# Moving all SBUF tiles of a two-block transformer kernel: first address 17,408 instead of 16,512

## The reference

```python
hx = modulate(rmsnorm(x, norm1_g), mx[0], mx[1])      # mx, mc = silu(c) @ ada_w + ada_b
hc = modulate(rmsnorm(ctx, norm1_g), mc[0], mc[1])
ux, uc = hx @ w_in, hc @ w_in                         # 1024 -> 5120
sc_f, sc_b = gated scan states of the context         # from uc
ox = gated scan of ux in both directions, from these states
ya = fourier_mix(ux[:512]) @ w_a
yb = readout(ux, ox) @ w_b
x = x + mx[2] * ((sigmoid(ga) * ya + sigmoid(gb) * yb) @ w_out)
h2 = modulate(rmsnorm(x, norm2_g), mx[3], mx[4])
z = depthwise_conv3x3(h2 @ ffn_up) + conv_b           # 1024 -> 5632, on a grid of 4 x 64
x = x + mx[5] * ((silu(z[:2816]) * z[2816:]) @ ffn_down)
x = rmsnorm(x, final_g)
```

```python
p = rms_norm(x, norm1_g_2) @ w_in_2                   # 1024 -> 2560
q, k = rms_norm(q), rms_norm(k)
mix = [softmax attention with a bias, gated short convolution, windowed means]
x = x + mix @ w_out_2
f = square(relu(rms_norm(x, norm2_g_2) @ w_mlp1))     # 1024 -> 4096
x = x + f @ w_mlp2
```

## The kernel before

| tile | address | modulo 1,024 | modulo 64 |
|---|---|---|---|
| `raw0` | 16,512 | 128 | 0 |
| `whi0` | 49,280 | 128 | 0 |
| `wlo0` | 73,856 | 128 | 0 |
| `XR` | 98,432 | 128 | 0 |
| `vec` | 113,280 | 640 | 0 |
| `RR` | 121,696 | 864 | 32 |
| `base` (all areas) | 123,872 | 992 | 32 |

## Time and profile before

### The profile page before, as it was taken

How to read it: one execution, slowest core, us unless ns; L and a number is a source line. 1 busy time by engine, 2 the same in 40 slices (tenths; PEclk the granted TensorE clock), 3 DMA queues, 4 the chain that set the end, 5 groups by cost and what they waited for, 6 DMA issues and landing times.

```text
span 762.5 us, 14142 instructions
## 1 busy us (share of the span) xinstructions
PE 739.1 (97%) x5852; PEld 717.0 (94%) x5852; DVE 491.2 (64%) x907; ACT 358.6 (47%) x452; POOL 398.5 (52%) x223
## 2 busy tenths in 40 slices
PE   7779999999999989999999999999899999999998
PEld 3679889999999989999999999999899999999997
DVE  3877797569526559777777764548655656556553
ACT  5586224245434555554555546346454433334331
POOL 0767553546648957878878877766585300000000
PEclk9999999999999989999999999999999999999999
DMA  9984886337534437555455544433435464464411
GB/s 362 417 360 162 344 304 262 140 111 244 207 110 159 166 117 294 177 188 200 167 170 199 184 167 166 166 112 111 148 133 203 181 220 165 169 216 160 176 57 56
DMA packets 21089, 145.84 MB, mean 191 GB/s; under 512 B 2465, under 2 KB 2977, under 8 KB 3746
## 3 DMA queue, kind: packets, MB, share of 16 engines
q1 hardware_dynamic: 20880, 144.87, 51.8%
q10 hardware_dynamic: 146, 0.07, 0.0%
HBM read 143.88 MB, written 1.05 MB: 190 GB/s over the span
## 4 chain that ended last, share of the span: by engine, by line
PE 90%; DVE 4%; ACT 4%; issue 2%; DMA 0%; DVEq 0%; ACTq 0%
PE bank L1426 24%; PE bank L1428 24%; PE bank L1427 24%; PE bank L1444 3%; PE CP L1428 2%; PE CP L1426 2%; PE CP L1427 2%; PE bank L1533 2%; PE bank L1469 1%; ACT SCR L793 1%; ACT whi L487 1%; PE bank L1484 1%; DVE GA L1119 1%; PE CP L1458 0%; PE bank L1642 0%
## 5 line engine op out<-in xcount | busy, mean ns | idle before, releaser
L469 POOL TENSOR_TENSOR wlo<-raw,whi 128x512 fp32r<-128x512 f32 (+1 forms) x201 | 377.8, 1910 | 170.6 <-ACT whi L487 170.5
L487 ACT ACTIVATE whi<-raw 128x2048 fp32r<-128x2048 f32 x103 | 196.3, 1907 | 43.7 <-PE bank L1428 29.2
L1186 DVE SCALAR_TENSOR_TENSOR Y<-bank,vec,Y 128x189 f32<-128x189 f32 (+2 forms) x352 | 123.0, 423 | 43.6 <-ACT Y L734 43.6
L1426 PE MATMUL bank<-H2h,whi 128*128 128x256 f32 x352 | 101.0, 287 | 1.7 <-DVE H2l L1161 1.7
L1427 PE MATMUL bank<-H2l,whi 128*128 128x256 f32 x352 | 100.6, 286 | 0.0
L1428 PE MATMUL bank<-H2h,wlo 128*128 128x256 f32 x352 | 99.8, 284 | 0.0
L1426 PE MATMUL bank<-H1h,whi 128*128 128x256 f32 (+1 forms) x288 | 90.9, 316 | 8.3 <-DVE H1l L917 4.5
L1428 PE MATMUL bank<-H1h,wlo 128*128 128x256 f32 (+1 forms) x288 | 89.2, 310 | 0.0
L1427 PE MATMUL bank<-H1l,whi 128*128 128x256 f32 (+1 forms) x288 | 89.0, 309 | 0.0
L850 DVE TENSOR_TENSOR wlo<-raw,whi 128x2048 fp32r<-128x2048 f32 x28 | 64.4, 2300 | 34.5 <-ACT whi L487 34.5
L1426 PE MATMUL bank<-H4h,whi 128*128 128x256 f32 x256 | 72.6, 284 | 0.0
(11 more groups left out here) (326 smaller groups left out, 1878.9 us busy)
## 6 DMA issues: line engine op xcount, KB each, us to landing
raw<-in_w_mlp SPq DMA_DIRECT2D x32, 1024.0 KB, 4.8
raw<-in_w_in SPq DMA_DIRECT2D x30, 1024.0 KB, 5.7
raw<-in_ffn_up SPq DMA_DIRECT2D x22, 1024.0 KB, 4.9
raw<-in_ada_hi SPq DMA_DIRECT2D x16, 1024.0 KB, 4.9
raw<-in_ffn_down SPq DMA_DIRECT2D x11, 1024.0 KB, 4.8
raw<-in_w_out SPq DMA_DIRECT2D x8, 1024.0 KB, 4.8
ada_s<-in_ada_s SPq DMA_DIRECT2D x4, 1024.0 KB, 18.1
ada_p<-in_ada_p SPq DMA_DIRECT2D x2, 1024.0 KB, 10.2
```

The costliest lines, as they stand in the source:

```text
L469: m = e.tensor_tensor(l[:, a:a + step], r[:, a:a + step], h[:, a:a + step].bitcast(F32), ALU.subtract)
L487: e.activation(whi[q % NHI][:, :], raw[n % NRAW][:, :], ACT.Copy).then_inc(s["w_hi"], 1)
L1186: e.scalar_tensor_tensor(o[:, r0:r1, c0:c1], z[:, r0 + dr:r1 + dr, c0 + dc:c1 + dc], cw[:, f, tap:tap + 1], o[:, r0:r1, c0:c1], ALU.mult, ...
L1426: e.matmul(out, h[:, col:col + P], xh, start=first, stop=False, skip_group_check=True)
```

## The change

`start` goes from 16,512 to 17,408, and `base` is rounded up to the next multiple of 1,024:

```diff
@@ -175,7 +175,7 @@
-    start = 16512
+    start = 17408
     cursor = [start]
@@ -216,7 +216,7 @@
     GS = keep("GS", [P, KT])
-    base = cursor[0]
+    base = (cursor[0] + 1023) // 1024 * 1024
```

## The result

| | before | after |
|---|---|---|
| median of 20 runs | 764.90 us | 767.86 us |
| range | from 763.85 us | 765.14 to 769.11 us |
| ratio of the runs | | 1.0032 [1.0026, 1.0039] |
| profiled execution, span | 764.52, 762.5 us | 765.14, 763.1 us |

The forecast was 732.8 us, with a range from 724 to 767 and 0.12 on slower. The time lies outside the range, on the other side of before. One run of before took 943.3 us and one beside the experiments 1,199.9 us; both are left out of what follows.

A forecast was written before the change was run, and what follows sets the result against it. PE bounds the kernel through the distance between matmuls. Gains of 29.0, 2.6 and 0.8 us less 0.5 for GpSimd sum to 31.9 us, taken from 764.5 or 764.9 to give 732.8 us; range 724 to 767.

The forecast's parts named there:

- What bounds the kernel: Whole kernel: PE, busy 739.1 of 762.5 us; matmul distance 120.0 ns, 13.3 of it set by the streaming operand's address.
- (a) Activations: Streamed tiles in mm3 and by_tokens: moving from 32 to 0 modulo 64 gains 29.0 + 2.6 + 0.8 us.
- seventeenth 64-byte block: Streaming reads: a run starting 32 bytes into a block touches 17 blocks, not 16, costing 6.7 ns per run.
- The 0.5 us taken back for GpSimd: Eight chunks of w_a, w_b and w_out: GpSimd's 5.50 us per chunk would bind against PE's 5.44, costing 0.5 us.
- (b) Weight buffers: Weight buffers and XR, moved by 896 bytes: bits this high show no effect on the pace, so nothing taken.
- (c) DMA: First 38 us, queues full: nothing taken, at most 2.5 us; the skill's 256-byte rule would give 1.2 us.
- (d) The other engines: VectorE, ScalarE, GpSimd: none but GpSimd at 233:268 near full in bound stretches; only softmax could show change; nothing taken.
- Rival 2: All matmuls: the change does nothing to PE, two reads cost 120.0 ns whatever their address; 764.9 us, chance 0.20.
- Rival 3: mm3: streaming and stationary reads collide when starting in step, about 125 ns; 21.7 us slower, 787 us, chance 0.12.
- Rival 1: mm3 and by_tokens: alignment helps only to by_tokens' pace, 117.3 ns for both streams; 752 us, chance 0.13.

The follow-up runs named there:

- e9: The changed kernel with GpSimd's last chunk (w_mlp1 3) given to VectorE and base 64 bytes back; median 743.70 us, ratio 0.9714.
- e8: The changed kernel with GpSimd's last chunk (w_mlp1 3) given to VectorE and base 512 bytes on; 764.22 us.
- e12: The changed kernel with GpSimd's last chunk (w_mlp1 3) given to VectorE and base 256 bytes on; 765.98 us.
- e3: The kernel before with only base rounded up, by 32 bytes to 123,904, start left at 16,512; 764.26 us, ratio 1.0000.
- e1: The changed kernel run once more, nothing else altered; 768.10 us, ratio 1.0041.
- e16: The kernel before with start 16,544 and base 96 bytes behind the last tile, last chunk left with GpSimd; median 751.73 us, ratio 0.9783.
- e2: The kernel before with only start moved to 17,408, base following unrounded; 764.92 us, ratio 1.0002.

## Why the prediction was wrong

**What bounds the kernel** was right: PE, by the distance between starts, 120.0 ns where 106.7 are columns. That the address of the streaming operand sets it was right in kind. e9 shows what was there to win: 2.9%, with 113.3 ns in all but some 140 us of its profiled execution.

**(a) Activations, -32.4 us: the step that failed.** I laid a line through two overheads (13.3 for one run, 20.0 for two), read its slope as a seventeenth 64-byte block, and let it go with the shift. Two points always lie on a line, and nothing in the trace tested the reading: all tiles shared one offset. The measured terms are 4,346 x 0.0 = 0 us for the 256-column form, 192 x -6.6 ns = -1.3 us for the 512-column form (forecast -2.6), and 192 x +2.6 ns = +0.5 us for the bound `by_tokens` (forecast -0.8). 0.8 us of gain in place of 32.4. I had written that if the 512-column form did not fall by twice as much, the picture was wrong; here one fell and the other did not move. The 0.5 us taken back for GpSimd in 233:268 did not arise either, there being no faster PE to wait for it.

**(b) Weight buffers, nothing.** "Bits this high show no effect" looked at 128 against 640, which differ by 512. That difference is indeed without effect (e8, e12). But the shift was by 896, which is 128 modulo 256, and the streams moved by 1,056, which is 32: D went from 96 to 0 modulo 256. I priced the two shifts one by one where only their difference counts. That the time still came out near nothing is because 96 and 0 both give 120.0 ns (as 128 does in part, e3).

**(c) DMA, nothing.** Right. 364 and 416 GB/s became 366 and 420, the shares 0.90 and 1.00 for 0.91 and 1.01. 1% on 38 us is 0.4 us at most. The Trainium skill's rule on 256 bytes (DMA: Bandwidth & Descriptors, "How a descriptor splits into AXI transactions") would have given 1.2 us. The traces of before and after do not show it. That section speaks of bytes that are fetched from below the start, and the change moved only the side in SBUF, where the rows are written; the estimate passed over that.

**(d) The other engines, nothing.** This is the second failed step, and the sign of the result hangs on it. I looked for engines that are full over a stretch. The loss lies in a stretch where GpSimd works for 35.67 of 212 us: 2.1 us at one hand-over, and in e1 1.5 more at the lower clock behind it, less the 1.5 and 0.9 us that the profiles of after and e1 are ahead by then. The medians differ by 3.0, e1's span by 2.7. The earlier trace rows give a mean for 168 pieces; that mean does not say how long four take when VectorE works beside them.

**The rivals.** Rival 2 (nothing happens to PE, 764.9) is the one that came true for the pace, with 0.20. Its reason, a cost of two reads whatever their address, did not hold: e9 against e8 is 20 us by an address alone. The Trainium skill's lines of 16 bytes (SBUF — State Buffer, "Door 1: The DMA port swizzle") let me expect no change between two multiples of 16. There was none here, but the addresses of e8 and e9 are multiples of 16 too, so these lines do not explain the pace. Rival 3 (the two reads meet) had the right pair, streaming against stationary, but wanted 125 ns at a common start, where it is 120.0; I gave it a sign, and none of the eight distances is slower than 120.0. Rival 1 had `by_tokens` as the pace of both; it moved itself.

**The range.** Its upper end, 767, was the noise above rival 2, and the time is 0.9 above it. No case of mine held a loss of 0.3% by a mishap of order between two engines.

## To carry over

Where PE's pace is above one column per cycle, scan the distance between the streaming and the stationary tiles in steps of 32 bytes over 256 before explaining it, with several executions of each, since one distance can have two paces. One number in the placement was worth 2.9% here, and the two roles of a tile see it with opposite signs. The best version measured is before with three edits:

```diff
-    by_pool = [name not in ("w_mlp1", "w_mlp2") or name == "w_mlp1" and i < 4 for name, i in split]
+    by_pool = [name not in ("w_mlp1", "w_mlp2") or name == "w_mlp1" and i < 3 for name, i in split]
...
-    start = 16512
+    start = 17408
...
-    base = cursor[0]
+    base = (cursor[0] + 1023) // 1024 * 1024 - 64
```

And an edit that adds and removes nothing still moves every instruction by some tens of ns: where two engines that hinder one another start within that time of each other, and one of them feeds the bound engine, take the meeting out before measuring anything of this size.

## What the runs showed that I had not expected

- `mm3` of float32r, 128 x 256, runs at 113.3 to 120.0 ns by the distance of its operands, at the same clock; one execution can hold two of these paces, and a wait of 0.2 us at full clock can lie between them (e9, e16).
- Four GpSimd pieces of 512 columns take 5.94 or 8.04 us, and the same VectorE instruction 1.81 or 0.69 us, by who starts first within about 40 ns (before, e2, after, e1).
- A wait of PE of 1.94 us can be followed by 3.4 us at the lower level of the clock (e1) or by none (the profile of after).
